# Doubling the slot spacing of the second group's output projection and queries in a hybrid RWKV-7 / attention / PEER decoder step

## The reference, cut to what matters

```
m   = sigmoid(gA) * (A @ w_up_a) + sigmoid(gB) * (B @ w_up_b)
x1  = layer_norm(alpha * x + g1 * (m @ w_o))
h2  = x1 * (1 + sc2) + sh2
q   = (h2 @ peer_wq).reshape(n, 8 heads, 2, 128)
s1, s2 = q[:, :, 0] @ keys1.T, q[:, :, 1] @ keys2.T      # 128 keys each
idx, gate = the 16 best of the 16 x 16 sums of the best of s1 and s2, softmax
y   = layer_norm(alpha * x1 + g2 * sum_k gate_k * gelu(h2 . u_tab[idx_k]) * v_tab[idx_k])
```

## Time and profile before

| | before |
|---|---|
| median of 3 runs | 2636.25 us (2630.53 to 2638.31) |
| time of the profiled execution | 2635.76 us |
| its span in the trace | 2634.1 us |
| PE, DVE, ACT, POOL busy | 79%, 64%, 11%, 54% of the span |
| moved by DMA | 792 MB, of them 681 MB by POOL's queue |

### The profile page before, as it was taken

How to read it: one execution, slowest core, us unless ns; L and a number is a source line. 1 busy time by engine, 2 the same in 40 slices (tenths; PEclk the granted TensorE clock), 3 DMA queues, 4 the chain that set the end, 5 groups by cost and what they waited for, 6 DMA issues and landing times.

```text
span 2634.1 us, 31846 instructions
## 1 busy us (share of the span) xinstructions
PE 2093.9 (79%) x10266; PEld 860.4 (33%) x10266; DVE 1697.7 (64%) x3928; ACT 298.1 (11%) x646; POOL 1413.5 (54%) x1559
## 2 busy tenths in 40 slices
PE   4999799858888867768889689867777777776778
PEld 3444344433444446733224134311111111111112
DVE  2389898546543343587676775467777867777754
ACT  2112122221111121101100111100000000000000
POOL 0133333104333300277776775577777777777774
PEclk7899899979999978889999999999999999999999
DMA  7476767538565544599999999899999999999997
GB/s 265 128 255 226 251 233 235 165 115 327 189 196 168 188 161 144 208 345 407 405 403 385 375 380 358 283 377 409 409 363 372 376 380 369 363 379 357 383 408 289
DMA packets 264140, 792.05 MB, mean 301 GB/s; under 512 B 33209, under 2 KB 64669, under 8 KB 263481
## 3 DMA queue, kind: packets, MB, share of 16 engines
q0 software_dynamic: 191008, 680.63, 69.9%
q1 hardware_dynamic: 72992, 109.61, 12.1%
HBM read 779.03 MB, written 11.09 MB: 300 GB/s over the span
## 4 chain that ended last, share of the span: by engine, by line
POOL 31%; issue 11%; PE 9%; DMA 3%; DVE 2%; PEld 0%; ACT 0%; PEldq 0%; ACTq 0%; POOLq 0%; DVEq 0%
POOL arena L882 31%; PE bank L1446 5%; DMA arena<-in_peer_v,arena 3%; PE bank L1417 2%; PE bank L1393 1%; DVE arena L2481 1%; PE bank L1429 0%; PE bank L1461 0%; PEldq L1498 0%; PEld bank L1487 0%; DVE arena L2438 0%; PEld bank L1446 0%; PE bank L907 0%; ACT L1728 0%; DVE arena L2441 0%
## 5 line engine op out<-in xcount | busy, mean ns | idle before, releaser
L1446 PE MATMUL bank<-arena 128*32 128x512 f32 x2048 | 939.4, 607 | 314.3 <-DMA arena<-in_peer_v,arena 314.0
L2481 DVE CUSTOM_DVE_ANT_0 arena<-arena 128x1024 f32<-128x1024 f32 x512 | 624.7, 1222 | 362.9 <-DMA arena<-in_peer_u,arena 359.6
L882 POOL DMA_INDIRECT arena<-in_peer_u,arena x520 | 562.0, 1081 | 334.2 <-issue 151.8
L882 POOL DMA_INDIRECT arena<-in_peer_v,arena x520 | 574.5, 1105 | 208.3 <-issue 149.3
L1446 PEld LDWEIGHTS bank<-arena 128*32 128x32 f32 x2048 | 179.6, 110 | 987.5 <-DMA arena<-in_peer_v,arena 599.9
L907 PE MATMUL bank<-arena 128*128 128x128 f32 (+8 forms) x1528 | 388.6, 411 | 44.0 <-DMA arena<-in_w_up_a 12.0
L865 POOL DMA_DIRECT2D arena<-in_cache_k x256 | 137.5, 537 | 345.4 <-issue 225.9
L907 PEld LDWEIGHTS bank<-arena 128*128 128x128 f32 (+3 forms) x1528 | 242.6, 192 | 193.5 <-issue 139.3
L865 POOL DMA_DIRECT2D arena<-in_cache_v x256 | 137.3, 536 | 307.4 <-issue 173.5
L1508 ACT ACTIVATE arena<-bank 128x512 f32<-128x512 f32 (+13 forms) x362 | 155.5, 430 | 1269.5 <-PE bank L1461 380.1
L1892 DVE TENSOR_TENSOR arena<-arena 128x512 f32<-128x512 f32 x256 | 175.2, 685 | 66.1 <-ACT arena L1508 47.6
(11 more groups left out here) (283 smaller groups left out, 1724.0 us busy)
## 6 DMA issues: line engine op xcount, KB each, us to landing
arena<-in_cache_k POOLq DMA_DIRECT2D x256, 256.0 KB, 3.9
arena<-in_cache_v POOLq DMA_DIRECT2D x256, 256.0 KB, 3.9
arena<-in_w_ada SPq DMA_DIRECT2D x12, 2048.0 KB, 12.0
arena<-in_w_in SPq DMA_DIRECT2D x10, 2048.0 KB, 12.1
arena<-in_peer_wq SPq DMA_DIRECT2D x16, 1024.0 KB, 13.2
arena<-in_peer_u,arena POOLq DMA_INDIRECT x520, 6.9
arena<-in_peer_v,arena POOLq DMA_INDIRECT x520, 6.7
arena<-in_w_o SPq DMA_DIRECT2D x8, 1024.0 KB, 14.1
```

The source lines that it names most:

```text
L882: nc.gpsimd.indirect_dma_start(gathered[:, j, :], None, tables[kind[0]][:, :], OFF(ap=index, axis=0)).then_inc(row_in[j], 16)
L1446: ins = mm(acc[u][32 * j:32 * (j + 1), :], spread[:, n % 2, b, :], gathered_row(("v", t, x))[:, 512 * u:512 * (u + 1)], start=x < 4, stop= ...
L2481: release(nc.vector.tensor_tensor_reduce(out=row, in0=row, in1=h2[:, t, :], scale=1.0, scalar=0.0, op0=MUL, op1=ADD, accum_out=gelu[:, at: ...
```

## The change

PE's halves of the second group's projection and query jobs are put two slots apart in place of one; ACT and DVE take the results at correspondingly later slots. A projection job takes four slots (48 in all, from slot 102 in place of 24 from slot 104), a head of the queries ten slots (from slot 180, last scores in slot 268, in place of five, 159 and 203). Norms and transposes move 20 slots later, with each one's length unchanged. ACT's root stays six slots ahead of the transpose. DVE's `projected` comes one slot after PE's second half, where it had been three slots after it.

```diff
 MIX_AT = 55
-OUT_AT = 104
-NORM_AT = (132, 140, 148)
-TURN_AT = (142, 150, 158)
-ASK_AT = 159
+OUT_AT = 102
+NORM_AT = (152, 160, 168)
+TURN_AT = (162, 170, 178)
+ASK_AT = 180
...
                     for i, t in enumerate(TILES[g]):
                         a, n = P * i, P if t < NT else NS
+                        yield from until(OUT_AT + 4 * (len(TILES[g]) * u + i))
                         o = begin(f"wo{g}_{u}_{t}")[0:n, 0:256]
                         for k in range(KD):
+                            if k == 4:
+                                yield from until(OUT_AT + 4 * (len(TILES[g]) * u + i) + 2)
                             ins = mm(o, mixed[:, k, a:a + n], w[:, k, :], start=k == 0, stop=k == KD - 1)
-                            if k == 3:
-                                yield
                         end(ins, f"wo{g}_{u}_{t}")
-                        yield
...
                     if h < PH:
-                        yield from until(ASK_AT + 5 * h)
                         w = late_weight(f"wq{g}_{h}")
                         for e in range(2):
+                            yield from until(ASK_AT + 10 * h + 4 * e)
                             o = begin(f"pq{g}_{2 * h + e}")[:, 0:span]
                             for k in range(KD):
+                                if k == 4:
+                                    yield from until(ASK_AT + 10 * h + 4 * e + 2)
                                 ins = mm(o, w[:, k, P * e:P * (e + 1)], h2_t[:, k, 0:span], start=k == 0, stop=k == KD - 1)
-                                if k == 3:
-                                    yield
                             end(ins, f"pq{g}_{2 * h + e}")
-                            yield
                     if h:
-                        yield from until(ASK_AT + 5 * h + 4)
+                        yield from until(ASK_AT + 10 * h + 8)
...
                         for e in range(2):
-                            yield from until(ASK_AT + 5 * h + 1 + 2 * e)
+                            yield from until(ASK_AT + 10 * h + 4 * e + 2)
                             take(f"pq1_{2 * h + e}", qp[:, h % 2, e, 0:span], bank(f"pq1_{2 * h + e}")[:, 0:span])
                     if h:
-                        yield from until(ASK_AT + 5 * h + 4)
+                        yield from until(ASK_AT + 10 * h + 8)
...
                     for i, t in enumerate(TILES[g]):
-                        yield from until(OUT_AT + 2 * (len(TILES[g]) * u + i) + 4)
+                        yield from until(OUT_AT + 4 * (len(TILES[g]) * u + i) + 3)
                         projected(t, u)
```

## The result

The changed kernel has a median of 2593.82 us over 4 runs (2588.99 to 2603.06), against 2633.39 us over 4 runs of the kernel before (2625.95 to 2638.31). The ratio is 0.9856, with a 95% interval of 0.9817 to 0.9895, so it is faster by some 28 to 48 us. The forecast was 2609 us with a range of 2597 to 2634: right in sign, 15 us too high, and the result lies 3 us under the low end.

What follows compares the result with a forecast made beforehand. Gathers set the pace generally, but PE bounds the second group's query stage. Slots 102 to 278 sum as 136.3 + 91.5 + 253.9 + 29.4 = 511.1 us, 27.7 less than 538.8, giving a 2609 us median, range 2597 to 2634.

Steps and rivals of the forecast that it cites:

- the ring: At DVE's wait for ACT's root in slot 200: buffered slots cover a wait of up to six slots.
- the nearest rows are slots 22 to 102, 2.84 us each, weights included: Projections, slots 102 to 150: rows set the pace, at the first group's 2.84 us a slot, giving 136.3 us.
- the 4 us for DVE's wait for the root: Queries, slots 180 to 268: allowance for DVE waiting on ACT's root in slot 200, between 0 and 8 us.
- the bytes alone: Slots 102 to 278: only bytes count, everything at 409 GB/s, 491 us, total 2588 us; chance 0.14.
- the cover is gone: Slots 102 to 278: POOL's slow gathers beside DVE set the pace, weights on top, 542 us, total 2639; chance 0.18.
- PE can't use the free slot: Projections and queries: v rows don't pile up, queries 3.2 us a slot, 557 us, total 2654 us; chance 0.05.

Runs made afterwards that it cites:

- the runs of the parts: Changed kernel with only projections spread, 2619.68 us; only queries spread, 2605.34 us; kernel before with norms, transposes and queries 20 slots later, no spacing changed, 2632.55 us.
- the run with seven slots: Changed kernel with seven slots for a head of the queries in place of ten, halves in slots 0, 1, 3 and 4, scores in 6: 2609.64 us.
- the run with the early root: Changed kernel with ACT's root for the output in slots 195, 323, 451 in place of 200, 328, 456, ahead of its score copies: 2601.76 us.
- the second set of runs: Changed kernel run again with no edit, for a second trace and a closer time: 2597.65 us median, ratio 0.9872 to the kernel before.

## Why the prediction was right in kind and wrong in size

**Right.** PE was the bound in the queries, rows and jobs in turn at 3.8 us a slot, and in the projections. The gain comes from the spacing: the runs of the parts show it (25 and 15 us, for 34 together, and at most some 5 for the place). In the queries POOL's wait for PE went from 40.2 us to none, the root's from 13.0 to 6.0 us (forecast under 8), six heads of queries took 173 us (170), at 400 GB/s (about 400). `weight_columns` of slot 278 started at 1872 us (1881). That rows go together when they pile up is shown by the run with seven slots. That DVE's stall is covered by the ring was half said (4 us were left for it); the run with the early root shows 1.4 us in the changed kernel.

**Wrong: the pace of the projections.** Piece by piece, forecast and measured in the first trace after:

| slots | forecast us | measured us |
|---|---|---|
| 102 to 150 | 136.3 | 130.3 |
| 150 to 182 (norms, two slots of queries) | 97.3 | 101.0 |
| 182 to 262 (queries) | 230.8 | 226.2 |
| 262 to 278 | 46.7 | 45.5 |
| all | 511.1 | 503.1 |

The step that failed is "the nearest rows are slots 22 to 102, 2.84 us each, weights included". I took a pace in us a slot over as if it were a property of the engines. In the projections it is bytes by rate, and the stretch that I took it from had more bytes in a slot and a lower rate. The DMA view of those 80 slots, in the kernel before:

```profile
GB/s 331 275 327 315 367 413 410 408 411 406 408 402 411 407 411 407 409 405 406 406 411 400 399 410 405 408 406 402 402 406 407 407 407 404 394 394 402 411 401 393
DMA packets 28234, 89.70 MB, mean 395 GB/s; under 512 B 2785, under 2 KB 6203, under 8 KB 28222
```

The first five of forty pieces, 28 us, are the start of the gathers at 275 to 367 GB/s, and the stretch held 1.121 MB a slot. The new projections held this, at the full rate:

```profile
DMA packets 16144, 52.94 MB, mean 406 GB/s; under 512 B 1590, under 2 KB 3780, under 8 KB 16138
```

52.94 MB in 130.3 us are 1.103 MB and 2.71 us a slot. The difference of 0.13 us, 6 us in 48 slots, is three quarters of the 8 us by which the sum was too high. "Weights included" was part of the miss: slots 22 to 102 held 7.73 MB of SP's transfers, the new projections 2.25 MB, since only two of the four loads of w_o fall into them.

The other pieces were off by less, and partly cancel. In the queries the same 2.84 held (2.83), but by luck: there a slot carries more bytes (90.54 MB in 80 slots, 1.132 MB each) at 400 GB/s. What was too high there is the 4 us for DVE's wait for the root. The norms were put 3.7 us too low: their 37.93 MB went at 375 GB/s, 7.6 us longer than at 406, beside the slow gathers named above.

The rival "the bytes alone" had the right mechanism for projections and queries, but put 409 GB/s everywhere and so gave 491 us. Worked out afterwards, the prediction's own bytes by the rates of the earlier trace rows, 406 GB/s for projections and queries and 367 for the norms, give 134 + 95 + 245 + 29 = 503 us. The total is right to the microsecond by luck: the pieces took 130, some 95, some 249 and some 29 us.

**Wrong: the anchor and the range.** Between the sum's 8 us and the 15 us on the median lie the median of before, which came down by 2.9 us with one more run, and scatter of the changed kernel's four runs (the second set of runs gave 2597.65, just inside the range). The range gave 12 us to the low side, although one execution of this kernel scatters by about 14 us, and although a rival of 0.14 lay at 2588. Its low end should have been near 2590. The rivals "the cover is gone" and "PE can't use the free slot" both fell: in the queries the gathers kept 400 GB/s with DVE at two thirds, and POOL's waits for PE went. What is left of the first of them are the slow gathers beside the norms, and the 371 to 381 GB/s behind slot 278.

**The rule on HBM.** The Trainium skill's page "DMA: Bandwidth & Descriptors", section "Where 436 GB/s comes from", has HBM bind at about 358 GB/s a core. The trace held 398 for 503 us on this one core, so the bound doesn't hold in this case.

## What to carry to other kernels

Where background work is written into a schedule of slots beside a stream of transfers, compare what the slowest engine needs in a slot with what the stream needs, and spread the work until it fits; beyond that nothing is gained (15 slots in place of ten), and quarters in every slot do nearly as well as halves in every second (4.3 us more). To price the stages after such a change, count the bytes of each and divide by the rate of the row that is most like it, without the start of the stream, in place of carrying over a time per slot. One rate for all of them isn't enough: 409 gave 491 us in the rival, and 406 for the 200.13 MB gives 493, against 503, because the norms don't reach it. And compare two kernels on the stretch that the edit moved: here it repeated within 4 us, while the untouched rest scattered by 19.

## What the runs showed of the hardware

One row's four matmuls (32 columns each) take 1.83 us between wide jobs. Two rows of different column parts that had both piled up take 1.85 us together between two wide jobs, and five take 3.62. PE runs them side by side only if nothing wide stands between them. So a job between rows costs more than its own time, and PE's busy share (97% before) hides it. The 1.85 us are the best case: in the changed kernel some 35 such pairs took 1.85 to 3.81 us, about 3.1 in the median, presumably because the second row often landed while the first was running.

The other thing is that 240 slots of gathers behind slot 278 take 654 to 673 us from execution to execution, at 371 to 381 GB/s. Some of the runs move a job in these slots, but the changed kernel alone gave 654.3 and 671.2 us in its two traces. The cause wasn't looked for and stays open.
